# Head projection in 128-token tiles, with the raw weights loaded in eight slices per block

## What is computed

```python
h = jnp.concatenate([meta, x], axis=1)          # 16 + 1024 rows
u = rms_norm(h, norm1_w[l])
proj = u @ w_in[l]                              # p_diff: 3 x 1024 columns
q = partial_rope(rms_norm(q, q_norm_w), pos)    # 8 heads x 2 x 64
k = partial_rope(rms_norm(k, k_norm_w), pos)
for s, e in bounds:                             # queries s:e against keys 0:e
    sc = jnp.einsum('bqhcd,bkhcd->bhcqk', q[:, s:e], k[:, :e]) * scale
...
return h[:, N_META:]
```

## Time and profile before

| what | value |
|---|---|
| time, median of three runs | 2773.99 us |
| lowest and highest of them | 2769.28 and 2774.26 us |
| span of the profiled execution, first to last instruction | 2770.1 us |
| the profiled execution's own time outside the span | not recorded; the three runs lie 0.8 us below to 4.2 us above the span |
| TensorE busy | 2617.0 us, 94% of the span |
| project_heads on TensorE, first matmul to the last one's slot | 430.08 to 777.95, 347.87 us |
| granted TensorE clock, mean | 0.986 |

### The profile page before, as it was taken

How to read it: one execution, slowest core, us unless ns; L and a number is a source line. 1 busy time by engine, 2 the same in 40 slices (tenths; PEclk the granted TensorE clock), 3 DMA queues, 4 the chain that set the end, 5 groups by cost and what they waited for, 6 DMA issues and landing times. The chain is left out here.

```text
span 2770.1 us, 66149 instructions
## 1 busy us (share of the span) xinstructions
PE 2617.0 (94%) x28073; PEld 2190.7 (79%) x28073; DVE 1563.2 (56%) x2377; ACT 1318.0 (48%) x2272; POOL 316.2 (11%) x367
## 2 busy tenths in 40 slices
PE   6999999999999999989999999999999999999992
PEld 5989897777766766678999998888888888888882
DVE  4566664443035555544444444553326888888884
ACT  4645552222134444334444444552223777777771
POOL 0111222332000000001212121100001000000002
PEclk9999999999999999999999999999998999999996
DMA  4344332222132323313221201154345999999976
GB/s 111 148 167 145 125 138 89 92 93 74 37 96 65 99 68 102 114 38 81 55 69 52 64 21 33 48 152 129 121 185 219 397 395 395 395 396 395 395 301 258
DMA packets 162649, 440.53 MB, mean 159 GB/s; under 512 B 16295, under 2 KB 96825, under 8 KB 150097
## 3 DMA queue, kind: packets, MB, share of 16 engines
q1 hardware_dynamic: 146413, 381.95, 38.7%
q10 hardware_dynamic: 9060, 29.56, 2.8%
q0 software_dynamic: 6912, 25.17, 2.4%
HBM read 344.22 MB, written 92.41 MB: 158 GB/s over the span
## 5 line engine op out<-in xcount | busy, mean ns | idle before, releaser
L2671 DVE TENSOR_TENSOR ex_wL<-wx,ex_wH 128x2048 fp32r<-128x2048 f32 x192 | 436.1, 2286 | 46.5 <-ACT ex_wH L2575 43.8
L2575 ACT CAST ex_wH<-wx 128x2048 fp32r<-128x2048 f32 x192 | 366.4, 1912 | 96.3 <-PE ex_bank L2467 70.7
L2465 PE MATMUL ex_bank<-ex_wH,ex_xTH 128*128 128x512 f32 x512 | 199.4, 389 | 0.6 <-DVE ex_xTL L2676 0.6
L2467 PE MATMUL ex_bank<-ex_wL,ex_xTH 128*128 128x512 f32 x512 | 199.3, 389 | 0.0
L2466 PE MATMUL ex_bank<-ex_wH,ex_xTL 128*128 128x512 f32 x512 | 199.2, 389 | 0.0
L717 PE MATMUL ph_acc<-ph_wH,uH 128*104 128x512 f32 x480 | 191.5, 399 | 0.0
L717 PE MATMUL ph_acc<-ph_wH,uL 128*104 128x512 f32 x480 | 188.8, 393 | 0.0
L717 PE MATMUL ph_acc<-ph_wL,uH 128*104 128x512 f32 x480 | 188.6, 393 | 0.0
L419 PE MATMUL pf_acc<-uH,pf_wH 128*128 128x348 f32 x648 | 160.7, 356 | 6.4 <-DVE pf_wL L541 6.4
L419 PE MATMUL pf_acc<-uL,pf_wH 128*128 128x348 f32 x648 | 138.9, 323 | 0.0
L419 PE MATMUL pf_acc<-uH,pf_wL 128*128 128x348 f32 x648 | 138.3, 322 | 0.0
(11 more groups left out here) (416 smaller groups left out, 6879.5 us busy)
## 6 DMA issues: line engine op xcount, KB each, us to landing
wx<-in_expert_w_gate SPq DMA_DIRECT2D x32, 2048.0 KB
wx<-in_expert_w_up SPq DMA_DIRECT2D x32, 2048.0 KB
wx<-in_expert_w_down SPq DMA_DIRECT2D x32, 2048.0 KB
s_y<-ex_y ACTq DMA_DIRECT2D x32, 512.0 KB, 10.0
fw<-in_w_in SPq DMA_DIRECT2D x27, 512.0 KB
hw<-in_w_in SPq DMA_DIRECT2D x6, 2048.0 KB, 10.1
s_qkT<-ph_stg ACTq DMA_DIRECT2D x4, 2080.0 KB, 7.0
mb_gt<-s_pT SPq DMA_DIRECT2D x16, 512.0 KB, 3.6
```

Source lines behind the costliest of these rows:

```text
L2465: nc.tensor.matmul(out, aH, bH, start=first, stop=False)
L2467: return nc.tensor.matmul(out, aH, bL, start=False, stop=last)
L2575: nc.scalar.copy(wH[:, w, part], raw(j, s)[:, part]).then_inc(w_high, 1)
L2671: nc.vector.tensor_tensor(wL[:, w, part], raw(j, s)[:, part], wH[:, w, part], ALU.subtract).then_inc(w_low, 1)
```

## The change

Tiles become TS = 128 tokens. Tokens 16 to 1,039 are NS = 8 tiles; query blocks have just these, key and value blocks have a ninth tile for the 16 meta tokens. The ninth tile is multiplied with 72 token columns as the stationary operand (tokens 0 to 71), and only 16 rows of its result are used further on. Units go from 60 to 52, query and key units from 40 to 34. The raw weights come in eight transfers of 256 KB for each block, each one sent for when its slice of `w` has been split, with a semaphore of its own. The eight splits of a block lie beside tiles 1 to 7, two of them beside tile 4. The loops of VectorE, GpSimd and SyncE are written out. The attention stage loads query columns 16 to 1,039 only, and the tables of the rope come in the new tiling.

```diff
-        w_ready = sem("ph_w_ready")
+        w_ready = [sem(f"ph_w_ready{k}") for k in range(KD)]
...
+        TILES = [NS if blk < NI else NS + 1 for blk in range(NB + 2)]
+        UNITS = [(blk, t) for blk in range(NB + 2) for t in range(TILES[blk])]
+        QK = sum(TILES[:NB])
+        rows = lambda t: TS if t < NS else META
+        where = lambda t: slice(META + t * TS, META + t * TS + TS) if t < NS else slice(0, META)
+        against = lambda t: where(t) if t < NS else slice(0, 72)
+        SLICES = {1: (0,), 2: (1,), 3: (2,), 4: (3, 4), 5: (5,), 6: (6,), 7: (7,)}
...
-            with sp.Fori(0, NB + 1) as i:
-                sp.wait_ge(low, KD * i + KD + OPEN)
-                sp.dma_start(w[:], w_v[:, :, bass.ds(i * 512 + DIFF_COL + 512, 512)]).then_inc(w_ready, 16)
+            for blk in range(1, NB + 2):
+                at = DIFF_COL + 512 * blk
+                for k in range(KD):
+                    sp.wait_ge(low, KD * (blk - 1) + k + 1 + OPEN)
+                    sp.dma_start(w[:, k], w_v[:, k, at:at + 512]).then_inc(w_ready[k], 16)
...
-                    last = nc.tensor.matmul(acc[:, slot, :], uu[:, k, t * TT:(t + 1) * TT], ww[:, b, k, :],
+                    last = nc.tensor.matmul(acc[0:toks.stop - toks.start, slot, :], uu[:, k, toks], ww[:, b, k, :],
...
-            if k == 0:
-                act.wait_ge(w_ready, 16 * blk + OPEN)
+            if blk > 0:
+                act.wait_ge(w_ready[k], 16 * blk + OPEN)
...
-                    last = nc.tensor.transpose(tp[:, x % 2, k * TT:(k + 1) * TT],
-                                               qn[:, x % 2, k * 128:(k + 1) * 128], c.ident[0:TT, 0:TT])
+                    last = nc.tensor.transpose(tp[:, x % 2, k * TS:k * TS + n],
+                                               qn[0:n, x % 2, k * 128:(k + 1) * 128], c.ident[0:n, 0:n])
...
-                if 1 <= t <= KD:
-                    split_high(act, 1 - blk % 2, blk + 1, t - 1)
+                for k in SLICES.get(t, ()):
+                    split_high(act, 1 - blk % 2, blk + 1, k)
...
-                sp.dma_start(q[:, s, :], c.qkT[h]).then_inc(loaded[s], 16)
+                sp.dma_start(q[:, s, META:], c.qkT[h, :, META:]).then_inc(loaded[s], 16)
```

More of the change, by code:

```diff
@@ L659, in project_heads @@
         wL = sb("ph_wL", [128, 2, KD, 512], F32R)
[L660 to L669, removed]
+        nw = sb("ph_norm_w", [TS, 2, DD])
+        cos = sb("ph_cos", [TS, NS + 1, ROPE])
+        sin = sb("ph_sin", [TS, NS + 1, ROPE])
+        sq = sb("ph_sq", [TS, 2, 512])
+        ms = sb("ph_ms", [TS, 2, G])
+        rs = sb("ph_rs", [TS, 2, G])
+        ri = sb("ph_ri", [TS, 2, G])
+        qn = sb("ph_qn", [TS, 2, 512])
+        ra = sb("ph_ra", [TS, G, ROPE])
+        rb = sb("ph_rb", [TS, G, ROPE])
         stg = sb("ph_stg", [128, 2, 4, T])
-        vst = sb("ph_vst", [TT, 2, 512])
-        acc = ps("ph_acc", [TT, 2, 512])
+        vst = sb("ph_vst", [TS, 2, 512])
+        acc = ps("ph_acc", [TS, 2, 512])
         tp = ps("ph_tp", [128, 2, 512])
@@ L733, in turn @@
             def turn(x):
+                n = rows(UNITS[x][1])
                 pe.wait_ge(roped, x + 1 + OPEN)
@@ L757, in stage @@
             def stage(x):
-                blk, t = divmod(x, NT)
-                b = blk % 2
+                blk, t = UNITS[x]
+                b, n = blk % 2, rows(t)
                 act.wait_ge(turned, x + 1 + OPEN)
@@ L762, in stage @@
                     act.wait_ge(stored[b], 16 * (blk // 2) + OPEN)
-                nc.scalar.copy(stg[:, b, :, t * TT:(t + 1) * TT],
-                               tp[:, x % 2, 0:4 * TT].rearrange("p (k t) -> p k t", k=4)).then_inc(staged, 1)
-                if t == NT - 1:
+                nc.scalar.copy(stg[:, b, :, where(t)],
+                               tp[:, x % 2, :].rearrange("p (k t) -> p k t", k=4)[:, :, 0:n]).then_inc(staged, 1)
+                if t == TILES[blk] - 1:
+                    first = META if blk < NI else 0
                     act.wait_ge(staged, x + 1 + OPEN)
-                    act.dma_start(c.qkT[4 * blk:4 * blk + 4].rearrange("k p t -> p k t"), stg[:, b]).then_inc(stored[b], 16)
+                    act.dma_start(c.qkT[4 * blk:4 * blk + 4, :, first:].rearrange("k p t -> p k t"),
+                                  stg[:, b, :, first:]).then_inc(stored[b], 16)
             for k in range(KD):
                 split_high(act, 0, 0, k)
-            for x in range(QK):
-                s = x % 2
-                blk, t = divmod(x, NT)
+            for x, (blk, t) in enumerate(UNITS[:QK]):
+                s, n = x % 2, rows(t)
                 act.wait_ge(product, x + 1 + OPEN)
-                nc.scalar.activation(sq[:, s, :], acc[:, s, :], ACT.Square).then_inc(sq_done, 1)
+                nc.scalar.activation(sq[0:n, s, :], acc[0:n, s, :], ACT.Square).then_inc(sq_done, 1)
                 act.wait_ge(ms_done, x + 1 + OPEN)
-                nc.scalar.activation(rs[:, s, :], ms[:, s, :], ACT.Sqrt, bias=c.eps[0:TT, :],
+                nc.scalar.activation(rs[0:n, s, :], ms[0:n, s, :], ACT.Sqrt, bias=c.eps[0:n, :],
                                      scale=1.0 / DD).then_inc(rs_done, 1)
@@ L780, in _ @@
                     stage(x - 1)
-                if 1 <= t <= KD:
-                    split_high(act, 1 - blk % 2, blk + 1, t - 1)
+                for k in SLICES.get(t, ()):
+                    split_high(act, 1 - blk % 2, blk + 1, k)
             stage(QK - 1)
-            for u in range(U):
-                b, t = divmod(u, NT)
+            for u, (blk, t) in enumerate(UNITS[QK:]):
+                n = rows(t)
                 act.wait_ge(product, QK + u + 1 + OPEN)
@@ L788, in _ @@
                     act.wait_ge(v_stored[u % 2], 16 * (u // 2) + OPEN)
-                nc.scalar.copy(vst[:, u % 2, :], acc[:, u % 2, :]).then_inc(v_copied, 1)
-                if b == 0 and 1 <= t <= KD:
-                    split_high(act, 1, NB + 1, t - 1)
+                slot = (QK + u) % 2
+                nc.scalar.copy(vst[0:n, u % 2, :], acc[0:n, slot, :]).then_inc(v_copied, 1)
+                if blk == NB:
+                    for k in SLICES.get(t, ()):
+                        split_high(act, 1, NB + 1, k)
                 act.wait_ge(v_copied, u + 1 + OPEN)
-                act.dma_start(c.vD[t, :, b * 512:(b + 1) * 512], vst[:, u % 2, :]).then_inc(v_stored[u % 2], 16)
+                act.dma_start(c.vD.rearrange("n p d -> (n p) d")[where(t), (blk - NB) * 512:(blk - NB + 1) * 512],
+                              vst[0:n, u % 2, :]).then_inc(v_stored[u % 2], 16)
             for s in range(2):
                 act.wait_ge(stored[s], 16 * NI + OPEN)
-                act.wait_ge(v_stored[s], 16 * (U // 2) + OPEN)
+                act.wait_ge(v_stored[s], 16 * (NS + 1) + OPEN)
         @block.vector
@@ L805, in _ @@
             dve.wait_ge(scaled, 1 + OPEN)
[L806 to L827, removed]
@@ new lines, in _ @@
+            ch = Chain(dve, vec)
+            for x, (blk, t) in enumerate(UNITS[:QK]):
+                s, n = x % 2, rows(t)
+                dve.wait_ge(sq_done, x + 1 + OPEN)
+                nc.vector.tensor_reduce(ms[0:n, s, :], sq[0:n, s, :].rearrange("p (g d) -> p g d", g=G),
+                                        AX.X, ALU.add).then_inc(ms_done, 1)
+                dve.wait_ge(rs_done, x + 1 + OPEN)
+                ch(nc.vector.reciprocal(ri[0:n, s, :], rs[0:n, s, :]))
+                if x >= 2:
+                    dve.wait_ge(turned, x - 1 + OPEN)
+                q3 = qn[0:n, s, :].rearrange("p (g d) -> p g d", g=G)
+                ch(nc.vector.tensor_tensor(q3, acc[0:n, s, :].rearrange("p (g d) -> p g d", g=G),
+                                           ri[0:n, s, :].unsqueeze(2).to_broadcast([n, G, DD]), ALU.mult))
+                nc.vector.tensor_tensor(q3, q3, nw[0:n, blk // NI, :].unsqueeze(1).to_broadcast([n, G, DD]),
+                                        ALU.mult).then_inc(normed, 1)
+                for k in SLICES.get(t, ()):
+                    split_low(dve, 1 - blk % 2, blk + 1, k)
@@ L833, in _ @@
             pool.wait_ge(tables, 64 + OPEN)
[L834 to L847, removed]
+            ch = Chain(pool, rope_step)
+            for x, (blk, t) in enumerate(UNITS[:QK]):
+                n = rows(t)
+                pool.wait_ge(normed, x + 1 + OPEN)
+                q3 = qn[0:n, x % 2, :].rearrange("p (g d) -> p g d", g=G)
+                h = ROPE // 2
+                cs = cos[0:n, t, :].unsqueeze(1).to_broadcast([n, G, ROPE])
+                sn = sin[0:n, t, :].unsqueeze(1).to_broadcast([n, G, ROPE])
+                ch(nc.gpsimd.tensor_tensor(ra[0:n], q3[:, :, 0:ROPE], cs, ALU.mult))
+                ch(nc.gpsimd.tensor_tensor(rb[0:n, :, 0:h], q3[:, :, h:ROPE], sn[:, :, 0:h], ALU.mult))
+                ch(nc.gpsimd.tensor_tensor(rb[0:n, :, h:ROPE], q3[:, :, 0:h], sn[:, :, h:ROPE], ALU.mult))
```

(8 more changed lines are left out.)

8 lines of the change are left out of this document (3 added, 5 removed).

## The result

| | before | after |
|---|---|---|
| time, median | 2773.76 us (4 runs) | 2731.28 us (4 runs) |
| lowest to highest | 2769.28 to 2774.26 | 2729.07 to 2737.65 |
| ratio after to before | | 0.9856, 95% interval 0.9843 to 0.9870 |
| span of the profiled execution | 2770.1 | 2735.9 |
| project_heads, first matmul to the last one's slot | 347.87 | 306.11 |

The medians differ by 42.5 us, and the interval of the ratio spans 36 to 43.5 us; 44.8 were forecast. The profiled execution of the kernel after is its slowest (2737.65 us, 1.75 us outside the span), so its span is not the place to look for the gain. The stage is.

The account below looks back on a forecast made before the run. TensorE's unbroken chain of matmul slots was taken to bound project_heads, its length a count times a slot. Terms -44.4 - 2.2 - 1.2 + 1.1 + 2.4 - 0.5 gave -44.8 us, so 2729 us; 8-in-10 range 2721 to 2739.

Parts of the forecast that it names:

- The step from the stage to the program: Barriers part the stages, so the program saves what project_heads saves unless later stages change their own work.
- Fewer units: project_heads on TensorE: 60 units become 52; 192 matmuls go, -44.4 us, and six groups of transposes, -2.2 us.
- Wider tiles: Matmul slot in project_heads: loading 128 columns instead of 104 has no visible price; slot 0.2305 instead of 0.2315, -1.2 us.
- Wider transposes and the double split: project_heads: transposes stream 128 columns, +1.1 us; two splits beside tile 4 delay GpSimd 0.6 us in four blocks, +2.4.
- Splits that end at tile 7: Blocks 0 and 1: slice 7 is split during the next block's first unit, with one us of room, 0.
- Eight transfers: Raw weights in project_heads: each slice requested a block ahead of its use, on a mostly idle queue, 0.
- The stage's end: End of project_heads: last store shrinks to 16 rows and can land sooner; between 0 and -0.8, taken as -0.5 us.
- The shorter slot: Rival in project_heads: wider tile brings the experts' slot of 0.2268, another 4.6 us go, 2724 us; chance 0.10.
- the load that shows: Rival: 20 ns more per full-tile weight load goes unhidden, +23 us, 2752; chance 0.05 shared with clock low in meta units alone.
- the clock that falls in meta units: Rival: half clock, slot up to 0.2315 us longer; meta units alone 2751, chance 0.05 shared; lasting longer 2796, chance 0.03.
- Waits that come back: Rival: chain from product to `roped` outgrows 0.1 us of room in all 34 units, or slice 7 late; 2744 us, 0.08.
- One sign of error: Prediction called wrong if a later stage changes its length by more than 3 us; other signs: slot above 0.2335, clock under 1.00.

Follow-up runs that it names:

- tiles_only: Kernel after, with a block's raw weights sent in one 2 MB transfer behind the last split instead of eight; median 2722.41 us, ratio 0.9862.
- slices_only: Kernel before, tiles still 104 tokens, with raw weights sent in eight 256 KB transfers per block; median 2762.14 us against 2759.45, ratio 1.0010.
- meta16: Kernel after, with 16 instead of 72 token columns as the stationary operand of the meta units; median 2721.34 us, ratio 0.9861.
- order_hlh: Kernel after, with the three products of a slice ordered high-high, low-high, high-low (token part first); median 2725.68 us, ratio 0.9864.
- rows_1056: Kernel after, with 1,056 instead of 1,044 columns for each slice of the token operands; median 2728.30 us, ratio 0.9867.
- single_splits: Kernel after, with one split beside each of tiles 0 to 7 and none doubled; median 2728.44 us, ratio 0.9867.
- after_again: Kernel after measured again without edit; median 2727.98 us against 2759.45 for the kernel before on that chip, ratio 0.9877.
- queries_nine: Kernel after, with the ninth (meta) unit computed for the two query blocks too; median 2740.30 us against 2764.66, ratio 0.9916.
- paired_splits: Kernel after, with a block's eight splits as four pairs beside tiles 1, 3, 5 and 7; one time, 2732.20 us.
- meta_short: Kernel after, with meta units multiplying only the first slice, 3 matmuls instead of 24 (results not the layer's); median 2717.45 us, ratio 0.9836.

## Why the prediction was right

*The bound.* TensorE's slots set the stage: the matmul count is exact, the stage fell by 41.8 us where 44.3 were forecast, and the two halves of the change tried alone (tiles_only, slices_only) gave all and nothing.

*The step from the stage to the program.* It held only in part, and the nearness of 42.5 to 44.8 is in part luck. The stage repeats; the program's gain over the kernel before measured beside it was 42.5 us in the first measurement and 31.5 in the second of this same kernel, 37.0 for tiles_only, 38.1 for meta16, 37.3 for order_hlh, 34.7 for rows_1056 and 34.6 for single_splits, whose stages are all 41 to 42 us shorter. The intervals are wide (24.8 to 43.0 us for after_again), but for rows_1056 and queries_nine the stage's gain lies outside them, by 0.4 and 0.8 us. In the six comparisons from the second measurement to single_splits about 4 to 10 us are missing, which the forecast put at nothing. Where they went is open. The table has rwkv 5.3 us longer in the kernel after, and 6.0 to 7.6 us longer in the three changed kernels than in slices_only on the same chip; but that was slices_only's fastest run, 5.4 us under its median.

*Fewer units, -44.4 and -2.2.* Held. queries_nine prices a unit with its transposes at 6.1 us, where the sum had 5.9.

*Wider tiles, -1.2.* The sign was wrong. The slot rose from 0.2315 to 0.2325 in the value units, +1.2 us over 1,248 matmuls, 2.4 away from the term and inside its bounds. Taking the attention row for its likeness was a guess. The rule from the Trainium skill ("TensorE: Matmul & The Clock Gate", section on LDWEIGHTS) held for the growth of the load, 20 ns from 104 to 128 columns; for the load itself it gives an estimate of 107 ns at 128 columns, where the trace has 188. As a cost the load did not show, neither at 128 columns nor, the other way, at 16.

*Wider transposes and the double split, +1.1 and +2.4.* Their sum is right, their parts are not. 34 groups cost 15.9 us; the terms gave 14.5 - 2.2 + 1.1 + 2.4 = 15.8. The double split costs 0.27 us, 1.1 in all: GpSimd gets its turn between two splits, and the cost lies in the middle between my bounds of 0 and 2.4. The rest is in the groups themselves. By the stage's means a usual unit is 6.01 - 24 x 0.232 = 0.44 us of transposes, where 0.364 + 0.04 was forecast: the streamed columns alone don't price them.

*Splits that end at tile 7, 0.* No wait in the kernel after. The room is 0.95 us, where 1.0 was read beforehand, and paired_splits uses it up.

*Eight transfers, 0.* Held. What hides them is more than I used: even one transfer of 2 MB fits between the last split of a block and the first of the next.

*The stage's end, -0.5.* It did not come: from the last slot to attention's first matmul there are 7.13 us before and 7.18 after. The last store is smaller, but the issue of attention's first load still follows it by 3.8 us (739.51 to 743.27):

```profile
739.51 0.32 ACTq L806 DMA_DIRECT2D s_v<-ph_vst  x1
```

```profile
743.27 0.33 SPq L956 DMA_DIRECT2D at_q<-s_qkT  x1
```

*The rivals.* The shorter slot, the load that shows and the clock that falls in meta units are refuted by the stage's rows and by meta16. Waits that come back are refuted for this kernel (7 waits of weight loads for GpSimd, 2.5 us in all, against 33 and 7.5 before); meta_short shows what that rival looks like when it does occur. Its half-clock slot of 0.43 us bears out the price of the clock rival, which took up to twice the slot. The trace of the kernel before has the same shape at that clock in the experts, four slots in 1.7 us (0.43 each) behind a pause of 2.05 us, so the price could have been read there:

```profile
2719.40:2721.10 1.70, 1.70 (x5) 0.50 1.01 417
```

*One sign of error did appear.* I named a later stage off by more than 3 us as a sign that the prediction is wrong. rwkv is 5.3 us longer in the profiled execution, and attention 3.0. One trace can't tell this from the spread: the same code of rwkv took 543.4 to 561.2 us in the six traces of the table, 551.0 in the second one of this same kernel. Why it varies was not tried, and the missing microseconds of the program leave open that a part of it belongs to the change.

## What to carry to other kernels

Where a matmul's slot is set by its streamed columns, the width of the stationary operand is free: count the units, fill the 128 columns, and leave out rows that nobody reads. Before a remainder unit is made shorter, look at the chain that follows the unit ahead of it: when that chain is as long as a unit, a short one turns into a wait, and the wait into matmuls at half clock. Compare the stage that was changed from trace to trace, and put the other stages' spread beside it before a span is read as a gain. Then measure the whole program more than once: here the stage gained 42 us each time and the program 31 to 43.

## What was not expected of the hardware

- A matmul that streams 512 columns takes 0.231 to 0.233 us from start to start in this stage with 16, 72, 104 or 128 stationary columns, though its load lasts from 95 (16 columns, meta16) to 188 ns (128).
- The same shape has a slot of 0.2268 us in one stage and 0.2333 in another at the same granted clock; the order of the products moved it by 0.0004 here and the row length of the stationary operand not at all, and within the experts it is 0.231 behind a pause and 0.227 a little later.
- After 4.54 us without a matmul, TensorE ran at a granted clock of 0.51 in the next 3.5 us, with slots of 0.43 us.
- GpSimd's first rope operation takes 0.45 to 0.47 us alone and 0.78 beside one of VectorE's splits (0.84 in the kernel before), and with two splits in a row its second takes 0.65 in place of 0.32.
